# Smaller first transfers, releases by ScalarE, merge sums in the bank and a gate projection in three pieces

## The reference, cut

```python
def reference(x, ...):
    h = rms_norm(x, norm_mix)
    (hq, hf, hi, hg, nq, kc, vc, ksl, vsl, kwn, vwn, ngate, gate_a, gate_b) = split(h @ w_in)
    y_a = hgrn2_mixer(hq, hf, hi, hg, lower_bounds, hg_out_gain) @ w_branch_a
    y_b = nsa_mixer(nq, kc, vc, ksl, vsl, kwn, vwn, ngate, ...) @ w_branch_b
    mixed = sigmoid(gate_a) * y_a + sigmoid(gate_b) * y_b
    x = x + mixed @ w_out
    h = rms_norm(x, norm_mlp)
    return x + square(relu(h @ w_up)) @ w_down
```

## Time and profile before

| | us |
|---|---|
| median of 3 runs | 817.58 (817.57 to 817.68) |
| the profiled execution, its own time | 817.72 |
| its span in the trace | 815.9 |
| TensorE busy | 799.5 |
| GpSimd busy | 490.3 |
| VectorE busy | 414.9 |
| ScalarE busy | 193.9 |

### The profile page before, as it was taken

The page is one execution under the profiler, slowest core; times in us unless marked ns, Lnnn a source line. Parts: engine busy times, 40 slices in busy tenths (PEclk is TensorE's granted clock), DMA queues, the critical chain, the costliest instruction groups (busy, mean ns, idle before and its releaser), DMA issues.

```text
span 815.9 us, 12340 instructions
## 1 busy us (share of the span) xinstructions
PE 799.5 (98%) x4632; PEld 635.4 (78%) x4632; DVE 414.9 (51%) x565; ACT 193.9 (24%) x397; POOL 490.3 (60%) x324
## 2 busy tenths in 40 slices
PE   8999999998999999999999999999999999999998
PEld 6788877987778566567878888888888888888886
DVE  6696485834465454543887766672000376650000
ACT  5100753312411455545112122220000122210000
POOL 4656644567454565464666666666666666776663
PEclk9999999999999999999999999999999999999999
DMA  7334221233422100004223222223332233233320
GB/s 248 105 126 168 96 79 55 78 116 117 154 78 78 53 27 27 27 27 181 98 84 103 99 83 103 90 90 104 103 100 82 101 104 98 82 103 129 119 86 26
DMA packets 22973, 78.01 MB, mean 96 GB/s; under 512 B 2659, under 2 KB 2923, under 8 KB 22804
## 3 DMA queue, kind: packets, MB, share of 16 engines
q1 hardware_dynamic: 18864, 68.69, 24.8%
q10 hardware_dynamic: 4068, 8.75, 3.0%
HBM read 75.31 MB, written 4.21 MB: 97 GB/s over the span
## 4 chain that ended last, share of the span: by engine, by line
PE 90%; DVE 5%; POOL 2%; DMA 1%; issue 1%; ACT 1%; SPq 0%; DVEq 0%; POOLq 0%; ACTq 0%
PE bank L364 25%; PE bank L366 24%; PE bank L365 24%; PE bank L694 3%; PE bank L706 3%; PE bank L727 2%; PE bank L444 1%; PE bank L446 1%; PE bank L445 1%; DMA wraw<-in_w 1%; PE bank L388 1%; POOL wsp L294 1%; DVE f L1129 1%; PE bank L493 1%; PE bank L716 1%
## 5 line engine op out<-in xcount | busy, mean ns | idle before, releaser
L294 POOL TENSOR_TENSOR wsp<-wraw,wsp 128x1024 fp32r<-128x1024 f32 x126 | 309.6, 2457 | 10.5
L292 POOL TENSOR_SCALAR wsp<-wraw 128x1024 fp32r<-128x1024 f32 x126 | 136.6, 1084 | 255.7 <-PE bank L366 165.3
L364 PE MATMUL bank<-hhi,wsp 128*128 128x512 f32 x352 | 141.2, 401 | 7.3 <-POOL wsp L294 2.5
L365 PE MATMUL bank<-hlo,wsp 128*128 128x512 f32 x352 | 137.4, 390 | 0.0
L366 PE MATMUL bank<-hhi,wsp 128*128 128x512 f32 x352 | 137.3, 390 | 0.0
L364 PE MATMUL bank<-ghi,wsp 128*128 128x512 f32 x256 | 100.3, 392 | 0.0
L366 PE MATMUL bank<-ghi,wsp 128*128 128x512 f32 x256 | 99.7, 390 | 0.0
L364 PE MATMUL bank<-uhi,wsp 128*128 128x512 f32 x256 | 99.7, 389 | 0.0
L365 PE MATMUL bank<-glo,wsp 128*128 128x512 f32 x256 | 99.7, 389 | 0.0
L365 PE MATMUL bank<-ulo,wsp 128*128 128x512 f32 x256 | 99.6, 389 | 0.0
L366 PE MATMUL bank<-uhi,wsp 128*128 128x512 f32 x256 | 99.6, 389 | 0.0
(11 more groups left out here) (241 smaller groups left out, 1024.5 us busy)
## 6 DMA issues: line engine op xcount, KB each, us to landing
wraw<-in_w SPq DMA_DIRECT2D x127, 512.0 KB, 3.2
x<-in_xT SPq DMA_DIRECT2D x4, 512.0 KB, 7.5
bias_skewed<-bias_lines ACTq DMA_DIRECT2D x1, 2048.0 KB
bias<-bias_skewed ACTq DMA_DIRECT2D x1, 2048.0 KB, 9.0
x<-in_xT ACTq DMA_DIRECT2D x1, 2048.0 KB, 8.4
out<-x ACTq DMA_DIRECT2D x8, 256.0 KB, 2.0
cst<-in_w ACTq DMA_DIRECT2D x1, 96.0 KB
ohs<-in_oh ACTq DMA_DIRECT2D x1, 82.5 KB
```

The costliest lines, as they stand in the source:

```text
L292: pool.tensor_scalar(whi[:, two, :], wraw[:, raw, :], 1.0, 0.0, ALU.mult, ALU.add).then_inc(w_hi, 1)
L294: pool.tensor_tensor(wlo[:, two, :], wraw[:, raw, :], whi[:, two, :].bitcast(F32), ALU.subtract).then_inc(w_split, 1)
L364: pe.matmul(out_, wh, mh, start=first, stop=False)
L365: pe.matmul(out_, wh, ml, start=False, stop=False)
```

## The change

1. **Transfers and splitting at the start.** x comes in five transfers of 1, 1, 2, 2 and 2 tiles, chunk 1 in four quarters. GpSimd splits chunk 0 in halves. ScalarE, not GpSimd, rounds chunk 1 (by quarters) and chunk 2; GpSimd does their low parts. The statistic of x moves from projection 2 to projection 3.
2. **Statistics' banks** are released by ScalarE behind its logarithm, no longer by VectorE.
3. **Around `ga0`**: `mixed_values(2)` moves ahead of `fold_hidden(1)`; ScalarE's sigmoid of `gs` moves ahead of `gelu_exp(1)`; VectorE copies `vc` before the product `gs`.
4. **Attention**: scores, shift and `invert` of tile 0 before `gb1`; `invert(t)` before a gate; `gb7` in pieces of 2, 4 and 2 groups after t = 32, 33 and 34, its gate behind the last evacuation.
5. **Merge**: product a and the sum are written into the bank of y_a; ScalarE and `mix_low` read them there. TensorE's first half of round n waits for `mix_lo`, the second for `y_read`.

```diff
+GB7_AT = {32: (0, 2), 33: (2, 6), 34: (6, 8)}
...
+X_PARTS = [(0, 1), (1, 2), (2, 4), (4, 6), (6, 8)]
...
+            for n, (a, b) in enumerate(X_PARTS):
+                sp.dma_start(x0[:, a:b, :], xT[:, a:b, :]).then_inc(x_in[n], 16)
             for n in range(4):
-                sp.dma_start(x0[:, 2 * n:2 * n + 2, :], xT[:, 2 * n:2 * n + 2, :]).then_inc(x_in[n], 16)
-            for c in range(1, FIRST):
+                q = slice(256 * n, 256 * n + 256)
+                sp.dma_start(wraw[:, 1, q], w[1, :, q]).then_inc(w1_in[n], 16)
+            for c in range(2, FIRST):
...
+            pool.wait_ge(w_landed[0], 16)
             for half in range(2):
                 c = slice(512 * half, 512 * half + 512)
-                pool.tensor_scalar(whi[:, 1, c], wraw[:, 1, c], 1.0, 0.0, ALU.mult, ALU.add).then_inc(
+                pool.tensor_scalar(whi[:, 0, c], wraw[:, 0, c], 1.0, 0.0, ALU.mult, ALU.add).then_inc(
                     half_split, 1)
                 pool.wait_ge(half_split, 2 * half + 1)
-                pool.tensor_tensor(wlo[:, 1, c], wraw[:, 1, c], whi[:, 1, c].bitcast(F32), ALU.subtract).then_inc(
+                pool.tensor_tensor(wlo[:, 0, c], wraw[:, 0, c], whi[:, 0, c].bitcast(F32), ALU.subtract).then_inc(
                     half_split, 1)
             pool.wait_ge(half_split, 4)
             pool.sem_inc(w_hi, 1)
             pool.sem_inc(w_split, 1)
-            for c in range(2, AT["gb2"] + 1):
+            for n in range(4):
+                q = slice(256 * n, 256 * n + 256)
+                pool.wait_ge(w1_hi, n + 1)
+                pool.tensor_tensor(wlo[:, 1, q], wraw[:, 1, q], whi[:, 1, q].bitcast(F32), ALU.subtract).then_inc(
+                    w1_lo, 1)
+            pool.wait_ge(w1_lo, 4)
+            pool.sem_inc(w_hi, 1)
+            pool.sem_inc(w_split, 1)
+            pool.wait_ge(w2_hi, 1)
+            pool.sem_inc(w_hi, 1)
+            pool.tensor_tensor(wlo[:, 0, :], wraw[:, 2, :], whi[:, 0, :].bitcast(F32), ALU.subtract).then_inc(w_split, 1)
+            for c in range(3, AT["gb2"] + 1):
                 split_straight(c)
 
...
+            def w_quarter(k):
+                if k % 2 == 0:
+                    pe.wait_ge(w1_lo, k // 2 + 1)
...
-            first_projection(2, x_stat)
-            first_projection(3, lambda k: None)
+            first_projection(2, lambda k: None)
+            first_projection(3, x_stat)
...
+            pe.wait_ge(csum, 1)
+            mixed_values(2)
             fold_hidden(1)
             project("ga0")
             stat("st_o0", ones[:], sq[:, 0, :])
             pe.wait_ge(csum, 2)
-            mixed_values(2)
...
+            pe.wait_ge(cs_shift, ST)
+            scores(0)
+            project("gb1")
...
+            def part_of_gb7(k0, k1):
+                wh, wl = take("gb7")
+                to = claim("gb7") if k0 == 0 else bank_of("gb7")
+                for k in range(k0, k1):
+                    c = slice(k * P, k * P + P)
+                    last = three(to[:], wh[:, c], wl[:, c], hhi[:, k, :], hlo[:, k, :], k == 0, k == KT - 1)
+                if k1 == KT:
+                    last.then_inc(w_used, 1)
...
+                if t in GB7_AT:
+                    part_of_gb7(*GB7_AT[t])
...
-                    if n >= 2:
-                        pe.wait_ge(y_read, 2 * (n - 2) + j + 1)
+                    if n >= 2 and j == 0:
+                        pe.wait_ge(mix_lo, n - 1)
+                    if n >= 2 and j == 1:
+                        pe.wait_ge(y_read, 2 * (n - 2) + 2)
...
+                if name != "stat_x":
+                    act.sem_inc(free[USE[name] % 2], 1)
...
+                q = slice(256 * n, 256 * n + 256)
+                act.wait_ge(w1_in[n], 16)
+                act.activation(whi[:, 1, q], wraw[:, 1, q], ACT.Copy).then_inc(w1_hi, 1)
+            act.wait_ge(w_landed[2], 16)
+            act.wait_ge(w_used, 1)
+            act.activation(whi[:, 0, :], wraw[:, 2, :], ACT.Copy).then_inc(w2_hi, 1)
...
-            gelu_exp(1)
             act.wait_ge(decayed, 9)
             act.wait_ge(gs_out, HG)
             act.activation(e[:], gs[:], ACT.Sigmoid).then_inc(g_sig, 1)
             act.preload_act_table_set("natural_log_exp_and_others")
+            gelu_exp(1)
...
-                act.activation(hhi[:, n, :], rstd[:, n % 2, :], ACT.Copy).then_inc(mix_hi, 1)
+                act.activation(hhi[:, n, :], bank[2 + 2 * n % 4][:], ACT.Copy).then_inc(mix_hi, 1)
...
-            dve.wait_ge(g_sig, 1)
-            link(dve.scalar_tensor_tensor(gs[:], gs[:], g_hg, e[:], ALU.mult, ALU.mult))
-
             dve.wait_ge(cmp_out, 2)
             link(dve.tensor_copy(vc[:].rearrange("p g d -> p (g d)"), bank_of("cmp_v")[:, 0:P]))
             dve.sem_inc(vc_ready, 1)
             leave_stat("cmp_v")
+            dve.wait_ge(g_sig, 1)
+            link(dve.scalar_tensor_tensor(gs[:], gs[:], g_hg, e[:], ALU.mult, ALU.mult))
 
...
+            shift(0, 0)
+            shift(0, 1)
+            invert(0)
+            gate("gb1")
...
-                if 1 <= t <= NT:
+                if 2 <= t <= NT and t - 1 not in GB_AFTER:
                     invert(t - 1)
-                if t < NT:
+                if 0 < t < NT:
                     shift(t, 1)
                 if LAG <= t < NT + LAG:
                     evacuate(t - LAG)
                 if t >= VALUES + 7 and (t - VALUES - 7) % 8 == 0:
                     out_low((t - VALUES - 7) // 8)
                 if t in GB_AFTER:
-                    gate(GB_AFTER[t])
+                    if t < NT:
+                        invert(t)
+                    if GB_AFTER[t] != "gb7":
+                        gate(GB_AFTER[t])
+                if t == NT + LAG - 1:
+                    gate("gb7")
                 if t == NT:
...
-                dve.tensor_tensor(hlo[:, n, :], rstd[:, n % 2, :], hhi[:, n, :].bitcast(F32),
+                dve.tensor_tensor(hlo[:, n, :], bank[2 + 2 * n % 4][:], hhi[:, n, :].bitcast(F32),
                                   ALU.subtract).then_inc(mix_lo, 1)
 
             for n in range(KT):
                 dve.wait_ge(gate_sig, 2 if n < 4 else 4)
                 dve.wait_ge(w_used, AT[f"ab{n}"] + 1)
-                if n >= 2:
-                    dve.wait_ge(mix_lo, n - 1)
-                for j in range(2):
-                    dve.tensor_tensor(gates[:, j, n, :], gates[:, j, n, :], bank[2 + (2 * n + j) % 4][:],
-                                      ALU.mult).then_inc(y_read, 1)
+                y_a, y_b = bank[2 + 2 * n % 4], bank[3 + 2 * n % 4]
+                dve.tensor_tensor(y_a[:], gates[:, 0, n, :], y_a[:], ALU.mult).then_inc(y_read, 1)
+                dve.tensor_tensor(gates[:, 1, n, :], gates[:, 1, n, :], y_b[:], ALU.mult).then_inc(y_read, 1)
                 dve.wait_ge(y_read, 2 * n + 2)
-                dve.tensor_tensor(rstd[:, n % 2, :], gates[:, 0, n, :], gates[:, 1, n, :], ALU.add).then_inc(mix_f, 1)
+                dve.tensor_tensor(y_a[:], y_a[:], gates[:, 1, n, :], ALU.add).then_inc(mix_f, 1)
                 if n:
                     mix_low(n - 1)
             mix_low(KT - 1)
```

More of the change, by code:

```diff
@@ L185, in build_block @@
         w_used = sem("w_used")
-        x_in = [sem(f"x_in{n}") for n in range(4)]
+        x_in = [sem(f"x_in{n}") for n in range(len(X_PARTS))]
+        w1_in = [sem(f"w1_in{n}") for n in range(4)]
+        w1_hi, w1_lo, w2_hi = sem("w1_hi"), sem("w1_lo"), sem("w2_hi")
         consts_in, small_landed = sem("consts_in"), sem("small_landed")
@@ L671, in c_turn @@
                 last.then_inc(cpT_done, 1)
-            c_scores(0)
-            for qb, name in enumerate(("ga5", "ga6", "ga7", "gb0")):
-                project(name)
-                c_turn(qb)
-                if qb < ST - 1:
-                    c_scores(qb + 1)
-            project("gb1")
             keys = (ksn, kwn)
@@ L695, in scores @@
                               start=True, stop=True).then_inc(s_done[g], 1)
+            c_scores(0)
+            for qb, name in enumerate(("ga5", "ga6", "ga7", "gb0")):
+                project(name)
+                c_turn(qb)
+                if qb < ST - 1:
+                    c_scores(qb + 1)
+            pe.wait_ge(cs_shift, ST)
+            scores(0)
+            project("gb1")
             def turn(t):
@@ L742, in _ @@
                     values(done // 4, done // 2 % 2)
-                if t in GB_AFTER:
+                if t in GB_AFTER and GB_AFTER[t] != "gb7":
                     project(GB_AFTER[t])
+                if t in GB7_AT:
+                    part_of_gb7(*GB7_AT[t])
             pe.wait_ge(oa_lo, HG)
@@ L848, in _ @@
             act.wait_ge(small_landed, 16)
+            for n, (a, b) in enumerate(X_PARTS):
+                act.wait_ge(x_in[n], 16)
+                for k in range(a, b):
+                    act.activation(hhi[:, k, :], x0[:, k, :], ACT.Copy, scale=g_mix[:, k:k + 1]).then_inc(x_hi, 1)
             for n in range(4):
-                act.wait_ge(x_in[n], 16)
```

(5 more changed lines are left out.)

22 lines of the change are left out of this document (8 added, 14 removed).

## The result

| | before | after |
|---|---|---|
| median, us | 817.55 (817.30 to 817.68, 6 runs) | 834.71 (833.61 to 836.18, 6 runs) |
| the profiled execution, us | 817.72 | 834.02 |
| its span, us | 815.9 | 832.2 |
| mean granted clock of TensorE | 1.00 | 0.989 |

The ratio is 1.021, with a 95% interval of 1.0197 to 1.0223: the change made the kernel 2.1% slower. The forecast was 827.6 with a range up to 833.3; the direction was right, the time lay 1.4 us above the range.

What follows compares the result with a forecast made beforehand. TensorE, busy 799.5 of 815.9 us, was taken as the bound. 817.72 - 2.8 - 0.6 - 2.9 - 1.3 - 1.0 + 18.6 = 827.7, or 827.6 against the median; range 824.8 to 833.3.

Steps and rivals of the forecast that it cites:

- The pause: Merge: TensorE waits for VectorE's products, sum and low part before `ab2` to `ab7`; six pauses of 3.1 us, cost 18.6.
- rival 2: Merge: the sum stays slow because operand `gates` is still in SBUF; 841.6 us, chance 0.06.
- The clock: Merge: TensorE's granted clock stays full at 1.00 despite the pauses; a fall was given chance 0.06.
- the sign: Merge: matmuls longer than 0.39 us behind the pauses would show that the clock fell.
- rival 3: Merge: the clock falls in the pauses; 860 us, or 844 if it recovers in mid-chunk; chance 0.06.
- The start: First projections: three waits and their restarts go; gain 2.8 us, bounds 0 and 2.8, upper end taken.
- Banks released by ScalarE: Statistics' banks: TensorE's wait of 0.6 at line 388 goes; gain 0.6 us.
- Around `ga0`: Waits for `hraw`, the split of `ga0` and at `ga1` go; gain 2.9 us, bounds 1.9 and 3.0.
- the third wait: At `ga1`: TensorE's 0.92 us wait for VectorE's bank release, which ScalarE now does; counted within the 2.9 around `ga0`.
- Scores of tile 0 before `gb1`: Attention: moves work under work, since TensorE does not wait there for scores; 0 us, bounds -0.3 and 0.4.
- `gb7` in pieces and `wo0`: Waits of 0.35 and 0.92 at `gb7` covered, gain 1.3 us; wait for the last low part at `wo0`, gain 1.0.
- Rivals 1 and 4: 1: pause absent, kernel faster, 809.0, chance 0.04; 4: gains at start and around `ga0` partly fail, 833.3 at most, chance 0.08.

Runs made afterwards that it cites:

- Experiment 3: The changed kernel with 13 matmuls of ones into an idle bank ahead of each of TensorE's six waits in the merge: 825.86 us, ratio 1.0095.
- 11: The changed kernel with 6 matmuls of ones into a free bank ahead of each of TensorE's six waits in the merge: 825.94 us, ratio 1.0085.
- experiment 6: The changed kernel with VectorE's low part of row n-1 between round n's products and sum, and ScalarE rounding row 0 earlier: 828.18 us, ratio 1.0120.
- experiment 8: The kernel before with only the statistics' banks released by ScalarE: 814.60 us, ratio 0.9957.
- experiment 9: The changed kernel with `mix_low(n-1)` ahead of round n's products, ScalarE's row 0 rounding earlier, and tile 0's scores back behind `gb1`: 806.94 us, ratio 0.9853.

## Why the forecast was right, and where it failed

**The pause: right.** TensorE waits six times, at the line and for the releaser that the forecast named, and one pause costs 3.14 where it said 3.1. The sum in the bank took 699 ns, not 2.8 us: rival 2 is false, and with it the doubt about one operand in SBUF. The low part with a source in a bank took 682 ns against 681 before, when its source was in SBUF. The Trainium skill ("VectorE: DVE Perf Modes", section on the TRN2 errata) has a PSUM source 62 cycles dearer; the low part's 682 against 681 ns shows no such difference.

**The clock: the step that failed.** The forecast set TensorE's clock as full in the merge and gave its fall 0.06, because pauses up to 1.5 us had left it full. A pause of twice that length was outside the trace, and the forecast said so; it should then have carried a real chance and the range should have reached it. The clock fell behind five of six pauses, and the sign that the forecast had named for it is there: matmuls of 0.63 us behind them. Experiment 3 shows that the idle stretch did it: with the pauses unchanged and filled, 825.9. The size that rival 3 gave, 844 for a recovery in mid-chunk, had 16.5 us for it, twice the 7.9 measured: it let half a chunk, 12 matmuls, run slow and counted six falls, where eight ran slow, five times. Without the falls the forecast's sum would have been some 1.6 too high: 827.6 against 826.1 by the table's terms and 825.9 by experiments 3 and 11. The Trainium skill ("TensorE: Matmul & The Clock Gate", section on why this matters for your kernels) says that gaps between bursts put the engine back to half rate; the trace agrees, with a granted clock of 0.53 in the window from 387.6, behind an idle stretch of 2.86 us. In experiment 6 stretches of 2.14 us were enough.

**The start: right,** 3.09 for 2.8, and 3.02 alone. Taking the upper end was justified.

**Banks released by ScalarE: under-sized,** 2.0 for 0.6. The forecast went by one wait in the list and passed over the pause that the view puts down to "issue"; experiment 8 shows that it goes too.

**Around `ga0`: right,** 3.18 for 2.9; 1.05 of it is the release (experiment 8), as the forecast said of the third wait.

**Scores of tile 0 before `gb1`: put at nothing.** The forecast called it work moved under work, with bounds of 0.3 lost and 0.4 gained; it cost 0.6, and experiment 9 gets the 0.6 back in its trace. It asked whether TensorE waits for scores, and not what the scores stood in front of: they had covered VectorE's release of a projection's bank.

**`gb7` in pieces and `wo0`: right,** 1.56 for 1.3 and 1.25 for 1.0.

The terms other than the merge came to 10.5 us against 8.6. That surplus hid part of the clock's cost, so the total was off by 7.1 only, which is luck. Rivals 1 and 4 did not come: no pause was absent, and none of the gains failed.

## What to carry to other kernels

When an edit moves a release from an early reader to a late one, look at what the late one stands behind on its own engine: here one instruction of VectorE, moved ahead of a wait (with one rounding of ScalarE moved up for it), turned 2.1% slower into 1.2% faster. When a new pause of TensorE is longer than any that the trace shows with a full clock, count the slow matmuls behind it as well as the pause. And read the pauses that the profile puts down to nothing; they can belong to the edit too.
